# Conditioning blocks summed over the chunks by VectorE beside the gated feed-forwards, instead of by TensorE

## What is computed

```python
sc, scc = silu(c), silu(c_ctx)                    # one vector of 1024 for each of two conditions
for l in range(2):                                # first kind: 9 blocks of conditioning per layer
    mod_l = split(sc @ w_ada[l] + b_ada[l], 9)    # w_ada[l]: 1024 x 9216
    mod_c = split(scc @ w_ada[l] + b_ada[l], 9)
    h  = ffn_half_step(h, mod_l[0:3], ...)        # "ffn1": gated, 1024 -> 2 x 2816 -> 1024
    h  = h + mod_l[5] * mixers(modulate(rms_norm(h), mod_l[3], mod_l[4]))
    h  = ffn_half_step(h, mod_l[6:9], ...)        # "ffn2"
    # and the same for the context hc with mod_c
for l in range(2):                                # second kind: 6 blocks per layer, c_2 and c_ctx_2
    x = x + g1 * mixers(rmsnorm(x) * (1 + sc1) + sh1)
    x = x + g2 * sq_relu_mlp(rmsnorm(x) * (1 + sc2) + sh2)
```

## Time and profile before

| | us |
|---|---|
| median of 3 runs | 3699.04 |
| lowest and highest | 3696.28, 3708.58 |
| the profiled execution, own time | 3709.28 |
| its span in the trace | 3707.3 |
| PE busy | 3551.2 (96%) |
| DVE busy | 1423.8 (38%) |
| ACT busy | 660.0 |
| chain that ended last: PE | 90% |
| bytes moved | 415.88 MB, mean 112 GB/s |

### The profile page before, as it was taken

The page is one execution under the profiler, slowest core; times in us unless marked ns, Lnnn a source line. Parts: engine busy times, 40 slices in busy tenths (PEclk is TensorE's granted clock), DMA queues, the critical chain, the costliest instruction groups (busy, mean ns, idle before and its releaser), DMA issues.

```text
span 3707.3 us, 43595 instructions
## 1 busy us (share of the span) xinstructions
PE 3551.2 (96%) x16180; PEld 2619.0 (71%) x16180; DVE 1423.8 (38%) x3435; ACT 660.0 (18%) x1299; POOL 24.1 (1%) x48
## 2 busy tenths in 40 slices
PE   7999998989999999999899999999899999999999
PEld 4888845556888888886558884444478885555888
DVE  3444512333444554553331001566155554244100
ACT  2000022541000010002351001333110001233100
POOL 0000000000000000000000000000000000000000
PEclk9999999989999999999899999999799999888999
DMA  6443231633222232224364444010132223110443
GB/s 228 153 155 138 89 112 46 219 130 114 91 86 85 83 123 91 85 85 150 140 247 165 152 148 153 29 57 17 40 120 91 85 86 142 51 57 17 165 153 108
DMA packets 112073, 415.88 MB, mean 112 GB/s; under 512 B 12352, under 2 KB 15552, under 8 KB 109760
## 3 DMA queue, kind: packets, MB, share of 16 engines
q1 hardware_dynamic: 104256, 376.49, 29.3%
q0 software_dynamic: 5312, 34.34, 2.6%
q10 hardware_dynamic: 2368, 3.10, 0.2%
HBM read 412.83 MB, written 1.05 MB: 112 GB/s over the span
## 4 chain that ended last, share of the span: by engine, by line
PE 90%; DVE 4%; ACT 2%; issue 2%; DMA 2%; SPq 0%; DVEq 0%; ACTq 0%
PE PS L738 26%; PE PS L791 16%; PE PS L671 11%; PE PS L825 10%; PE PS L1041 6%; PE PS L1032 3%; PE PS L603 2%; PE PS L1117 2%; PE PS L1099 2%; PE PS L863 2%; DMA ring<-stream 2%; PE PS L654 1%; PE PS L1108 1%; PE PS L1090 1%; PE PS L947 1%
## 5 line engine op out<-in xcount | busy, mean ns | idle before, releaser
L671 PE MATMUL PS<-xn,ring 128*128 128x256 f32 (+1 forms) x1664 | 421.3, 415 | 4.7 <-issue 4.5
L671 PEld LDWEIGHTS PS<-xn,ring 128*128 128x128 f32 x1664 | 316.1, 191 | 109.3 <-issue 71.4
L825 PE MATMUL PS<-arena,ring 128*128 (+2 forms) x1376 | 358.8, 424 | 1.3 <-DVE arena L2059 1.3
L825 PEld LDWEIGHTS PS<-arena,ring 128*128 128x128 f32 x1376 | 264.8, 193 | 93.7 <-issue 61.6
L738 PE MATMUL PS<-xn,ring 128*128 128x256 f32 x1312 | 302.1, 384 | 4.2 <-ACT xn L1247 2.5
L1041 PE MATMUL PS<-xn,arena 128*128 128x512 f32 (+1 forms) x640 | 283.5, 565 | 6.6 <-ACT mix L1431 5.2
L738 PEld LDWEIGHTS PS<-xn,ring 128*128 128x128 f32 x1312 | 248.1, 191 | 58.3 <-issue 19.0
L791 PE MATMUL PS<-xn,ring 128*128 128x256 f32 x752 | 223.7, 379 | 0.0
L791 PE MATMUL PS<-arena,ring 128*128 128x256 f32 x784 | 201.2, 379 | 0.0
L791 PE MATMUL PS<-xn 128*128 128x256 f32 x752 | 193.0, 379 | 0.0
L1041 PEld LDWEIGHTS PS<-xn,arena 128*128 128x128 f32 x640 | 114.9, 201 | 107.7 <-issue 94.7
(11 more groups left out here) (258 smaller groups left out, 4470.0 us busy)
## 6 DMA issues: line engine op xcount, KB each, us to landing
ring<-stream SPq DMA_DIRECT2D x716, 512.0 KB, 3.4
arena<-pair_m POOLq DMA_DIRECT2D x8, 1536.0 KB, 7.7
arena<-pair_n POOLq DMA_DIRECT2D x8, 1024.0 KB, 5.4
mix<-head_w POOLq DMA_DIRECT2D x16, 320.0 KB, 3.2
mix<-na_bias POOLq DMA_DIRECT2D x8, 512.0 KB, 3.6
mix<-masks POOLq DMA_DIRECT2D x1, 2048.0 KB, 8.1
h<-xT ACTq DMA_DIRECT2D x1, 1024.0 KB, 21.1
h<-ctxT ACTq DMA_DIRECT2D x1, 1024.0 KB, 33.0
```

Source lines behind the costliest of these rows:

```text
L671: m = pe.matmul(PS[:, bank, 0:tokens], ring[:, s, k * P:(k + 1) * P], xn[:, k, 0:tokens], start=k == 0, stop=k == DC - 1)
L825: m = pe.matmul(PS[:, out_bank(m_), 0:ph.tokens], ring[:, s, m_ * P:(m_ + 1) * P], rhs, start=isinstance(i, int) and k == 0, stop=True, sk ...
```

## The change

All blocks but the first two are computed another way. Their weights no longer come in `stream`: a second tensor `fed_w` holds them, and GpSimd loads its units into a ring of 4 slots (`fed_ring`, in a part of `arena` that the feed-forwards leave free), as `fed_used` frees them. DVE multiplies a unit by the condition's value of each partition and adds it to a running sum, for both conditions (`feed`: 16 instructions of 128 x 1024 for a block). When 8 units are summed, PE adds the partitions with `ones` as the stationary operand (`fed_sum`: 4 matmuls of 32 columns and 512, in place of 16), and turns as before (`fed_turn`).

Each of the four gated feed-forwards now feeds 7 blocks: 5 in its up phase (4 instructions of `feed` for each pair 1 to 20; the sum is added ahead of pairs 5, 9, 13, 17 and 21, the turn stands inside that pair) and 2 in its down phase, which PE adds in the norm behind it, with two turns in the first unit behind that. The other five norms, both `heads` loops and the sequence of 8 units in `swiglu` have none any more, and `swiglu` is written out without loops.

```diff
-        ada = 1 if shifted and (what, layer) != ("ffn1", 0) else 0
+        ada = FED_DOWN if plan[-1].kind in ("down", "down7") and plan[-1].which in ("ffn1", "ffn2") else 0
...
+                if ph.kind in ("up7", "swiglu") and ph.ada:
+                    last = PLAN[PLAN.index(ph) - 1]
+                    pool.wait_ge(norm_sum, last.at.sum + 1)
+                    first = (ph.at.ada - 1 - ADA_FIRST) * DC
+                    for u in range(first, first + (FED_UP + FED_DOWN) * DC):
+                        if u >= FED_RING:
+                            pool.wait_ge(fed_used, u - FED_RING + 1)
+                        pool.dma_start(fed_ring[u % FED_RING], fed_w[u]).then_inc(fed_in[u % FED_RING], 16)
...
+            def fed_sum(ph, block, bank, free):
+
+                pe.wait_ge(ada_done, free)
+                pe.wait_ge(fed_used, DC * (ph.at.ada - ADA_FIRST + block))
+                sums = fed_sums[(ph.at.ada - 1 - ADA_FIRST + block) % 2]
+                for q in range(4):
+                    m = pe.matmul(PS[32 * q:32 * q + 32, bank, :], ones[:, 0:32],
+                                  sums[q // 2][:, (q % 2) * 512:(q % 2 + 1) * 512], start=True, stop=True)
+                m.then_inc(ada_mm, 1)
...
                 if ph.ada:
                     pe.wait_ge(h_ready, ph.at.h)
-                    ada_units(ph, 0, 0, 0)
-                    ada_units(ph, 0, 2, 2)
+                    fed_sum(ph, 0, 5, ph.at.ada)
                 for n, q in enumerate(in_a_row(ph)):
                     pe.wait_ge(norm_rstd, q.at.rstd + 1)
                     spread(rstd[:, n, :], norm_spec(q).bank, q.tokens).then_inc(norm_spread, 1)
                 if ph.ada:
-                    ada_units(ph, 0, 4, 4)
-                    ada_units(ph, 0, 6, 6)
+                    fed_sum(ph, 1, 7, ph.at.ada)
...
+                for j in range(PAIRS):
+                    block = fed_block(ph, j)
+                    if block is None:
+                        pair(j)
+                    else:
+                        fed_sum(ph, block, FED_BANK, ph.at.ada + block)
+                        pair(j, lambda: fed_turn(ph, block, FED_BANK, 0, ph.at.ada + block))
...
-                    fill = (lambda k: None) if last else (lambda k: ada_units(ph, 0, k, k, i))
...
+                for j in range(PAIRS):
+                    dve.wait_ge(silu_done, ph.at.silu + j + 1)
+                    dve.wait_ge(acc_ready, ph.at.acc + 2 * j + 2)
+                    tt(hidden[:, j, 0:ph.tokens], PS[:, 2 * (j % 2) + 1, 0:ph.tokens], sa[:, j % 2, 0:ph.tokens],
+                       ALU.mult).then_inc(glu_done, 1)
+                    block = fed_block(ph, j)
+                    if block is not None:
+                        ada_add(ph, block, bank=FED_BANK)
+                    if 1 <= j <= 4 * ph.ada:
+                        feed(4)
...
+                    feeds = 2 if 1 <= j <= 4 * ph.ada else 0
+                    feed(feeds)
                     if j:
                         up7_mult(ph, j - 1)
-                    block, part = divmod(j - 2, 4)
-                    if part == 3 and 0 <= block < ph.ada:
-                        ada_add(ph, block, bank=ADA_BANKS_SEVEN[1])
+                    block = fed_block(ph, j)
+                    if block is not None:
+                        ada_add(ph, block, bank=FED_BANK)
+                    feed(feeds)
                     fold7(ph, j)
```

More of the change, by code:

```diff
@@ L162, in make_plan @@
         tiles = tokens // P
-        swiglu(l, "ffn1", TOK, 0 if l else 5)
+        swiglu(l, "ffn1", TOK)
         norm("mix", DC, TOK, 2, True, l)
@@ L328, in build @@
         ada_done = sem("ada_done")
+        fed_in = [sem(f"fed_in{r}") for r in range(FED_RING)]
+        fed_used = sem("fed_used")
         acc_ready = sem("acc_ready")
@@ L469, in unit_at, with fed_block @@
         def unit_at(ph, j):
-            return 2 * j + (2 * max(0, min(j - 1, 4 * ph.ada)))
+            return 2 * j
+        def fed_block(ph, j):
+            block, part = divmod(j - 2, 4)
+            return block if part == 3 and 0 <= block < ph.ada else None
         def made_at(ph, j, event):
@@ L749, in up7 @@
                     if j == 0 and last.ada:
-                        ada_turn(last, 0)
+                        norm_turns(last)
                 for name in ("P3", "P7"):
@@ L982, in iteration @@
                         turned(i, 3)
-                        if not last:
-                            ada_turn(ph, 0, i)
                     values(i, tiles - 1, last)
-                    if tiles == 2 and not last:
-                        ada_turn(ph, 0, i)
                 for t in range(2, 4):
@@ L1620, in swiglu @@
-                for j in range(head):
-                    pair(0, j)
-                with dve.Fori(0, U_SWIGLU // RING) as i:
-                    for j in range(RING // 2):
-                        if j == 3 and ph.ada:
-                            ada_add(ph, 0, i)
-                        pair(i, head + j)
+                for j in range(PAIRS):
+                    dve.wait_ge(silu_done, ph.at.silu + j + 1)
+                    dve.wait_ge(acc_ready, ph.at.acc + 2 * j + 2)
+                    tt(hidden[:, j, 0:ph.tokens], PS[:, 2 * (j % 2) + 1, 0:ph.tokens], sa[:, j % 2, 0:ph.tokens],
+                       ALU.mult).then_inc(glu_done, 1)
+                    block = fed_block(ph, j)
+                    if block is not None:
+                        ada_add(ph, block, bank=FED_BANK)
+                    if 1 <= j <= 4 * ph.ada:
+                        feed(4)
@@ L1754, in update @@
                             .then_inc(h_ready, 1)
+                feeds = 2 if ph.which != "mlp" else 0
                 for t in range(1, steps + 1):
                     down7_prep(ph, t)
+                    if t < steps:
+                        feed(feeds)
                 fold7(ph, 0)
@@ L1763, in down7 @@
                     down7_prep(ph, t)
+                    if t < steps + 8:
+                        feed(feeds)
                 for j in range(2, 4):
@@ L1778, in down @@
                 set_gate(ph)
+                if ph.which == "ffn2":
+                    feed(FED_DOWN * 2 * DC)
                 for m in range(DC):
@@ L2168, in ada_selector, with fed_selector @@
     return m
+def fed_selector():
+    m = np.zeros((P, 8), np.float32)
+    for q in range(4):
+        for j in (q // 2, q // 2 + 2):
+            m[32 * q, 4 * (q % 2) + j] = 1.0
+    return m
 def neighbour_bias(rpb):
@@ L2236, in layout @@
                         interleaved((w_ffn1_in if ph.which == "ffn1" else w_ffn2_in)[l]))
-            for j in range(ph.n):
-                block, part = divmod(j - 2, 4)
-                if 0 <= block < ph.ada:
-                    parts.append(ada[b + block, 2 * part:2 * part + 2])
-                parts.append(w[2 * j:2 * j + 2])
+            parts.append(w)
         if ph.kind == "down7":
```

179 lines of the change are left out of this document (86 added, 93 removed).

## The result

| | before | after |
|---|---|---|
| median of 5 runs, us | 3702.61 | 3735.13 |
| lowest and highest, us | 3696.28, 3708.58 | 3723.71, 3736.82 |
| profiled execution's span, us | 3707.3 | 3735.1 |
| ratio, 95% interval | | 1.0076, 1.0057 to 1.0095 |

The account below looks back on a forecast made before the run. The prediction took TensorE, busy 3551.2 of 3707.3 us, as the bound. Its terms -15 + 27 + 26 + 11 + 5 - 14 + 12 + 5 = +57 on 3699 gave 3756 us, range 3702 to 3785.

Parts of the forecast that it names:

- Steps 1 and 2: Up phases: five cheaper blocks in ffn1 of layer 0, -15 us; fifteen new blocks in the other three, +27 us.
- Step 3: `up7` and `down7`: VectorE's added sums fit beside its old work, 0 us; they cost from 1.45 us a sum.
- rival E: VectorE becomes the bound in `up7` and `down7` too, by slow sums or late units; 3780 us and more, chance 0.07.
- Step 4: Plain feed-forward (ffn2 of layer 1): TensorE waits 5.2 us for VectorE's multiplication and four sums, five times, +26 us.
- Step 5: Plain feed-forward: TensorE's clock falls behind the five new waits, 2.2 us each, +11 us.
- Step 6: `heads`: fourteen blocks removed free 28 us, the clock falling in two of three iterations costs 33; together +5 us.
- Step 8: Norm and `gates` of layers 3 and 2: slower clock less freed time, +12 us in layer 3 and +5 in layer 2.
- Step 7: Nine blocks out of the norms: seven norms not followed by `gates` gain 2 us each, -14 us.
- Step 9: The 224 new 512 KB loads through POOL cost 0 us, at worst half a sum's length of wait per block.
- Rival B: The clock falls in `heads` but not in `gates`: +36, 3735 us, chance 0.20.

Follow-up runs that it names:

- e1: Changed kernel with the plain feed-forward's (ffn2 of layer 1) four running sums put ahead of the pair's multiplication instead of behind it; 3689.10 us.
- e6: Changed kernel with running sums beside the seven-product feed-forwards cut to 64 columns from 1024, except a block's first two; 3735.92 us, one run.
- e2: Changed kernel with 16 matmuls on constants ahead of each `fed_sum`'s wait for `fed_used` in the plain feed-forward; 3722.67 us.
- e7: Changed kernel with two quarters' worth of unused matmuls ahead of the spread and two behind, in the norm ahead of layer 3's `gates`; 3729.87 us, one run.
- e3: Changed kernel with unused matmuls in each `heads` iteration's longest wait, 8 in layer 0 and 4 in layer 1; 3712.42 us.
- e8: Changed kernel with four quarters' matmuls on constants back in the `heads` loops, without loads or turn; 3745.64 us, one run.
- e10: Kernel before the change, with 2 us of unused matmuls at the start of the pairs of layers 2 and 3; 3699.39 us, 0.9991 of the kernel before.
- e5: Changed kernel with two of the plain feed-forward's four sums ahead of the multiplication and two behind; 3711.25 us, one run.

## Why the prediction was right in sign and too high

1. **Steps 1 and 2** (a block in `up7`). -15 and +27 were forecast. Measured: -17.5, and +17.0 in the two other `up7`; in the plain stage e1 leaves 165.31 - 154.60 = 10.7. 27.7 in all. Right.
2. **Step 3** (VectorE beside the seven products costs nothing). Right, by e6. Its threshold of 1.45 us a sum, which rival E uses as well, does not follow from its own numbers: (12.3 - 5.8) / 4 is 1.6. Measured were 1.28, under both.
3. **Step 4** (the wait behind the pair). 5.2 us each and 26 in all; measured 5.46 and 27.3. Most of the difference is the longer running sum: the four took 4.87 us (2009.79 to 2014.66) and not 4.72. e1 shows the mechanism: only the order was changed, and the wait was gone.
4. **Step 5** (the clock behind the waits). 11 was forecast; 10.8 by the windows and by e2 less the stage's start, 10.1 in e7's run. Right.
5. **Step 6** (`heads`). The first term held: -28 forecast, -31.5 by e3. The second was mis-sized: "I take two of three iterations: +33", and it is 19.9. I had taken the spread and the next score at half clock in each fallen iteration, 3.5 us. The rows show the clock low for the values and a part of the spread, and back before the score; the loss is 8.5 / 7 = 1.2 us an iteration in layer 0, and 11.4 / 7 = 1.6 in layer 1. The rule of the Trainium skill quoted there, in "TensorE: Matmul & The Clock Gate", section "HAM oscillation — how this bites in real kernels", that such a loop pays in every turn, fits layer 1, where the scores of successive iterations take 2.11, 3.21, 2.54 and 3.60 us instead of 1.96. It does not fit layer 0: the spread was slow in part in one iteration (2.67) and wholly in the next (3.62), and two of the seven iterations (within 629 to 649 and 711 to 731) ran at a clock of 1.00 although their wait was as long. The sum of the stage came out at -11.6 instead of +5: 17 us of the error.
6. **Step 8** (`gates`). This is the step that failed most: "I take 14 of clock". It cost 2.8, by e7, and the norm ahead gave back 1.6; layer 2 lost nothing in the clock (1.00 over the first 8 us of its unit), where the forecast had 7. I had read the earlier trace rows, 13 busy microseconds at 0.50 in the pairs, as if any busy stretch could stay there. But the unit of `gates` is other work than the pairs, and its clock was back 8 us after its start; no row of before showed this unit at half clock, and the rows of another stage were no bound for it. 19 us of the error.
7. **Step 7** (norms). -14 forecast, -14.9 measured. What it missed is the next stage: two turns in the first unit of the mixers' products, +1.8 and +4.4. In layer 0 one turn more is 0.9, and the rest is clock: it was 0.77 in the first 4 us of the stage, and 1.00 before. In layer 1 two pieces of `xn` came late within the stage (waits of 0.52 and 0.58 us) and the clock was 0.78 in the 4 us with the turns.
8. **Step 9** (DMAs). Right: 3.8 us to landing, and in e1 TensorE never waits for a load at 277 GB/s. The trace has one case in 224 that agrees with what the Trainium skill states in "SBUF — State Buffer", section "🔬 SBUF: two separate sides", that VectorE in a two-port mode holds up loads of GpSimd's queue. This issue came while VectorE was in the first multiplications of a block (scalar times tensor, 0.75 us each), and it took 1.15 us; the one behind it took 0.53, as all the others did, among them 80 beside running sums; no other issue met a first multiplication:

```profile
2194.45 1.15 POOL L578 DMA_DIRECT2D arena<-fed_w  x1 [1.86 <-DVE mix L1667]
2195.78 0.53 POOL L578 DMA_DIRECT2D arena<-fed_w  x1 [0.18 <-issue]
```

   Each of the ten traces with these loads has exactly one such issue, at the same place. TensorE did not wait for it, and rival E did not come.

Rival B, that the clock falls in `heads` and not in `gates`, gave 3735, the measured time. Its account of the places is right, but the number is in part luck, also because the median of the kernel before stands at 3702.61 in the comparison and not at 3699. Its sum was +36, and the two traces differ by 27.8: its `heads` were 17 us too high, and 6.2 in the mixers and 2.8 in the plain stage made up for part of that.

## What to carry to other kernels

Moving work to an engine that is idle most of the time is only free where the order of both engines lets it run early. Here the added sums stood behind an instruction that waits for TensorE, and TensorE's next instruction waited for the sums: 38 us from a place in the order, with VectorE busy 5.2 of 6.9 us. Put such work ahead of the wait, and look at what filled the waits before it is taken away. Work that ends before the wait would have ended cost nothing here and held the clock (e2, e3, e7). More work than that costs its time (e8), and work in a wait gives nothing where the next wait, for another engine, ends when it did (e10).

## What the runs showed of the hardware that I had not expected

- The same instructions can run at another granted clock from trace to trace. The pairs of layer 3 took 225.5, 236.0 and 237.0 us in three kernels that differ only in stages before (clock 0.88, 0.83, 0.82). Whether the earlier edits cause this is not shown, for there is one trace of each kernel, and traces differ ahead of any edit too: the changed kernel and e7 have the same instructions up to the norm of layer 3, and their `heads` of layer 1 took 141.4 and 143.5 us, their plain stages 203.4 and 199.8. So an edit of this size has to be read at its own place, up to the next wait for another engine, and not from the whole time or from a long stage behind it.
- Whether a wait of 3 us lowers the clock is not decided by its length alone: of the five waits of 3.07 us in e5, the first had 1.00 behind it, and the five together cost 8.0 us; of the seven of 2.8 us in layer 0's `heads`, two had.
- On GpSimd's queue one issue of a 512 KB load took 1.15 us instead of 0.53, in each of ten traces, and it was the only one that came while VectorE was multiplying a scalar by a tensor.
- A running sum (scalar times tensor plus tensor, 128x1024) took 1.277 us, 9% more than half of two plain products of the same size (1.18, with one operand in PSUM), and the first of a block (scalar times tensor) only 0.745.
